# Gated DeltaNet scan on one Trainium2 core: moving outside rows and state scalings from VectorE to GpSimd, and one gram product per direction

## The chip, the cores and the metric

The kernel runs on one core of one Trainium2 chip. The metric is device time in microseconds (us) for one execution of the whole program: both request groups (1024 and 256 tokens) through two layers. Lower is better. A core has TensorE (PE), VectorE (DVE), ScalarE (ACT), GpSimd (POOL) and SyncE (SP), whose queue issues the DMAs here. Each engine works through its own list of instructions in order, and semaphores make one wait for another.

## What is computed

An encoder trunk of two layers. The even layer mixes tokens with four gated DeltaNet heads (A, width 128) and eight RWKV-7 heads (B, width 64), each in both directions; the odd layer uses latent attention; each is followed by an MLP. The change lies in the scan of the even layer. The reference for A, per head, direction and chunk, cut to what matters:

```python
g = jnp.cumsum(g, axis=-1)
decay = jnp.exp(jnp.where(lower, g[..., :, None] - g[..., None, :], -jnp.inf))
L = jnp.where(strict, jnp.einsum('bhnik,bhnjk->bhnij', k_beta, k) * decay, 0.0)
sol = lax.linalg.triangular_solve(eye + L, rhs, left_side=True, lower=True)
u, w = sol[..., :DV], sol[..., DV:]
qk = jnp.einsum('bhnik,bhnjk->bhnij', q, k) * decay
...
v_new = u_c - w_c @ S
o = qd_c @ S + qk_c @ v_new
S = S * jnp.exp(gl_c)[..., None, None] + kd_c.T @ v_new
```

B carries a state of 64x64 per head that is multiplied by a decay per key column at each token and gets two outer products; the kernel also works it in chunks, with exponentials of summed decays on either side.

## The kernel before

All lines below are in `recurrences`, which works the scan in ten turns (`TILES` = 10), unrolled. Turn `i` handles token tile `i` forwards (direction 0) and tile `9 - i` backwards (direction 1), 128 tokens each.

**What a turn holds.** Six groups of four heads each: groups 0 and 1 are A in both directions, 2 to 5 are B. Each needs the inverse of a 128x128 unit triangular matrix per head. The inverse is built from blocks of 2 up to 128 in six levels; both directions of A share one set of tiles (quad 0), B has two sets (quads 1 and 2). For B the levels and quads give 12 units: `unit(u)` is level `u // 2 + 1` of quad `u % 2 + 1`. A unit runs as follows: PE makes Y from the current inverse (`y(u)`), ACT copies it from PSUM (`y_copy(u)`) and copies the inner blocks (`inner(u)`), PE makes the two products Z and ZT (`z(u)`), DVE puts their halves into the inverse (`joins(u)`: L2139, in the last level L2135 and L2136). PE runs `y(u+1)` before `z(u)`; `z(u)` waits for ACT's copy `y_copy(u)`.

**What is fitted between the units.** The lists of the engines are written out by hand. Behind `z(u)` PE does for A: `g_solve` (u = 1, 2), `g_outs` (3, 4), `g_state` for both directions and `g_sums` of the next turn (5), the second `g_sums` (6), the `gram` products (7, 8), and for B two `pairs` of K (9, 10). `g_sums` (L1522) multiplies a matrix of ones with `grow`, which GpSimd writes (L2050), one buffer for both directions: the second `g_rows` waits for the first `g_sums`. After the units come the first inverse of A for the next turn (`g_first`, GpSimd L2058, L2054, L2062, then PE L1569), `right`, `solve` and `outs` of B (PE L1702), between which A's first four levels for the next turn are done.

**The decay of A, before** (for the next turn, units 5 to 8). DVE's `shift` subtracts a row rate from the sums in PSUM (L2119) and adds `outside`, which is 0 inside and -1e9 outside the triangle (L2120). ACT's `decay_exp` takes the exponential in place (L1871). ACT's list has `inner(6)`, `y_copy(6)`, `decay_exp(0)`, `inner(7)`, `y_copy(7)`, `decay_exp(1)`, `inner(8)`, `y_copy(8)`. DVE's `gram` then multiplies, head by head, the K-K product with -beta and the decay into `NTc[0]` (direction 0) or `gY` (direction 1), four instructions at L2129, and the Q-K product with the decay into `A_o` in one (L2132). `gram_used` releases GpSimd's `g_first` and PE's later use of the banks.

**The states.** `S_g` (A) is multiplied by its last decay and gets PE's product, both on DVE (L2220, L2221), at units 5 and 6. `S_r` (B) is multiplied by `e_neg` before `right` reads it (L2252), between DVE's `k_masks(0)` and `k_masks(1)` ahead of unit 0, and by `rest` at the end of `outs` (L2234). DVE's other work here: `g_right` (L2203, L2204), `g_u` (L2208), `g_outs` (L2214 to L2216), `b_masks` (L2174, L2176), `k_masks` (L2183, L2184).

**Own waits.** The helper `Chain` (`link`) makes DVE wait for an instruction of its own that the next one reads. Its count per turn is `PER_DVE`, 40, and `DVE_BEFORE`, 11, ahead of the first turn.

**The prologue.** Ahead of the first turn the same decay and gram are done for turn 0. GpSimd clears tiles, copies the identity and, once all constants have been loaded, makes `first_level` (L2102), then `g_first`. PE waits for `gram_used` before the decay sums of B (L1535).

## Time and profile before

| | before |
|---|---|
| Three runs | 4106.44, 4113.89 (median), 4115.85 us |
| Profiled execution, its own time | 4113.53 us |
| Its span in the profile | 4111.7 us |
| Mean granted clock of TensorE | 0.965 |
| The scan, from its first memsets on GpSimd to the last turn's end | about 684 to 1462 us |
| A steady turn of the scan | 74.68 us |

Times in the rows further down are microseconds from the start of the span. A row of a timeline has the start, the duration, the engine, the line, the operation with output and inputs, the shapes, and the number of instructions put together; in brackets stands how long the engine had been idle and what ended that. Engines start an instruction before the one ahead has fully ended, so the spacing of two starts can be shorter than a duration. PE durations are modelled. Durations of groups elsewhere are means in nanoseconds.

### The profile page before, as it was taken

The page shows a single profiled execution, that of the slowest core. Times are in us where ns is not written, and L with a number is a line of the kernel's source. Part 1 is how long each engine was busy: PE and PEld are TensorE (multiplying, and loading weights), DVE is VectorE, ACT ScalarE, POOL GpSimd, SP SyncE. Part 2 cuts the span into 40 slices and gives each one's busy share as a digit, 9 for nine tenths or more (in the row PEclk, how much of TensorE's full clock was granted, in tenths as well). Part 3 has the DMA queues.
Part 4 walks back from the last instruction along what each step waited for, and adds up shares of the span by engine and source line. Part 5 has one row for each costly group of instructions (what it writes and reads, how often), then busy time and mean ns, then how long its engine had stood idle before and what let it go on. Part 6 is the DMA issues. An engine that isn't in the chain of part 4 may idle for free. (4 is left out here: it accounts for less than half of the span.)

```text
span 4111.7 us, 74086 instructions
## 1 busy us (share of the span) xinstructions
PE 3848.5 (94%) x31096; PEld 3274.5 (80%) x31096; DVE 2130.3 (52%) x3226; ACT 1300.7 (32%) x2303; POOL 897.4 (22%) x473
## 2 busy tenths in 40 slices
PE   7999886999999978999999997899979899999998
PEld 6888864888888867888888886788868788888887
DVE  5643256776777775443333346466643344333335
ACT  4321264444444444111111114255543211111112
POOL 1121065111111123111111112133322211111113
PEclk9999977999999989999999997999999999999999
DMA  4222387122222142011101113000022101110112
GB/s 122 91 77 82 112 289 258 64 78 70 64 90 69 44 175 98 31 41 41 39 32 41 41 41 113 8 7 7 1 77 93 50 32 41 41 39 33 41 41 103
DMA packets 205478, 289.17 MB, mean 70 GB/s; under 512 B 31216, under 2 KB 148144, under 8 KB 205248
## 3 DMA queue, kind: packets, MB, share of 16 engines
q1 hardware_dynamic: 205248, 285.82, 21.0%
q8 instruction: 179, 2.93, 0.3%
q14 instruction: 51, 0.42, 0.0%
HBM read 207.80 MB, written 77.99 MB: 70 GB/s over the span
## 5 line engine op out<-in xcount | busy, mean ns | idle before, releaser
L846 DVE TENSOR_TENSOR top_acc<-top_acc,ffn_down 128x512 f32<-128x512 f32 x600 | 412.1, 687 | 358.7 <-PE ffn_down L111 358.0
L109 PE MATMUL ffn_up<-hT_ffn_high,ffn_w_high 128*128 128x512 f32 (+1 forms) x1536 | 544.0, 354 | 4.9 <-DVE hT_ffn_low L808 4.9
L111 PE MATMUL ffn_up<-hT_ffn_high,ffn_w_low 128*128 128x512 f32 (+1 forms) x1536 | 544.0, 354 | 0.0
L110 PE MATMUL ffn_up<-hT_ffn_low,ffn_w_high 128*128 128x512 f32 (+1 forms) x1536 | 543.7, 354 | 0.0
L109 PE MATMUL ffn_down<-ffn_w_high,ffn_f_high 128*128 128x512 f32 x1280 | 498.6, 390 | 0.0
L110 PE MATMUL ffn_down<-ffn_w_low,ffn_f_high 128*128 128x512 f32 x1280 | 498.3, 389 | 0.0
L111 PE MATMUL ffn_down<-ffn_w_high,ffn_f_low 128*128 128x512 f32 x1280 | 497.9, 389 | 0.0
L835 DVE TENSOR_TENSOR ffn_square<-ffn_relu 128x512 f32<-128x512 f32 (+1 forms) x192 | 146.8, 764 | 640.8 <-ACT ffn_relu L761 640.8
L109 PEld LDWEIGHTS ffn_up<-hT_ffn_high,ffn_w_high 128*128 128x128 f32 x1536 | 290.5, 189 | 46.3 <-issue 5.3
L110 PEld LDWEIGHTS ffn_up<-hT_ffn_low,ffn_w_high 128*128 128x128 f32 x1536 | 290.5, 189 | 41.0
L111 PEld LDWEIGHTS ffn_up<-hT_ffn_high,ffn_w_low 128*128 128x128 f32 x1536 | 290.5, 189 | 40.0
L791 POOL TENSOR_TENSOR ffn_w_low<-up_w_raw,ffn_w_high 128x2048 fp32r<-128x2048 f32 x32 | 147.5, 4610 | 732.9 <-ACT ffn_w_high L767 720.4
L761 ACT ACTIVATE ffn_relu<-ffn_up 128x512 f32<-128x512 f32 (+1 forms) x192 | 101.1, 527 | 634.9 <-PE ffn_up L111 634.9
L753 ACT ACTIVATE ffn_w_high<-up_w_raw 128x2048 fp32r<-128x2048 f32 x32 | 61.4, 1917 | 745.5 <-DVE top_acc L846 695.8
L794 POOL TENSOR_TENSOR ffn_w_low<-up_w_raw,ffn_w_high 128x2048 fp32r<-128x2048 f32 x32 | 147.1, 4596 | 671.1 <-ACT ffn_w_high L753 671.1
L111 PEld LDWEIGHTS ffn_down<-ffn_w_high,ffn_f_low 128*128 128x128 f32 x1280 | 240.3, 188 | 50.2
L109 PEld LDWEIGHTS ffn_down<-ffn_w_high,ffn_f_high 128*128 128x128 f32 x1280 | 240.4, 188 | 49.3
L110 PEld LDWEIGHTS ffn_down<-ffn_w_low,ffn_f_high 128*128 128x128 f32 x1280 | 240.4, 188 | 48.6
L109 PE MATMUL project_bank<-hT_first_high,columns_w_high 128*128 128x512 f32 (+1 forms) x648 | 231.2, 357 | 5.9 <-ACTq L533 3.3
L110 PE MATMUL project_bank<-hT_first_low,columns_w_high 128*128 128x512 f32 (+1 forms) x648 | 230.8, 356 | 0.0
L111 PE MATMUL project_bank<-hT_first_high,columns_w_low 128*128 128x512 f32 (+1 forms) x648 | 230.4, 356 | 0.0
L3144 POOL TENSOR_TENSOR attend_w_sm<-attend_w_sm,attend_inv 128x1024 f32<-128x1024 f32 (+1 forms) x80 | 130.9, 1637 | 179.9 <-DVE attend_inv L3200 179.8
(476 smaller groups left out, 8025.4 us busy)
## 6 DMA issues: line engine op xcount, KB each, us to landing
up_w_raw<-in_w_ff SPq DMA_DIRECT2D x64, 1024.0 KB, 5.1
s_tm_both<-prepare_tb SPq DMA_DIRECT2D x20, 512.0 KB, 7.2
s_fm_dir<-prepare_fd SPq DMA_DIRECT2D x20, 512.0 KB, 5.8
scan_tb<-s_tm_both SPq DMA_DIRECT2D x20, 512.0 KB, 4.0
scan_fb<-s_fm_both SPq DMA_DIRECT2D x20, 512.0 KB, 4.9
scan_fd<-s_fm_dir SPq DMA_DIRECT2D x20, 512.0 KB, 5.2
up_w_raw<-s_x SPq DMA_DIRECT2D x20, 512.0 KB, 4.8
top_acc<-in_w_in_even SPq DMA_DIRECT2D x18, 512.0 KB, 5.4
```

What stands on the lines that cost most here:

```text
L109: pe.matmul(out, stationary[0], moving[0], start=start, stop=False)
L110: pe.matmul(out, stationary[0], moving[1], start=False, stop=False)
L111: return pe.matmul(out, stationary[1], moving[0], start=False, stop=stop)
L753: act.activation(w2_sb[0][:, :, :], w2_raw[:, :, :], ACT.Copy).then_inc(w2_high, 1)
L761: act.activation(relu[u % 2][:, 0:n], bank[u % 4][:, 0:n], ACT.Relu).then_inc(relu_done, 1)
L791: pool.tensor_tensor(w1_sb[1][:, :, :], w1_raw[:, :, :], w1_sb[0][:, :, :].bitcast(F32), ALU.subtract).then_inc(w1_low, 1)
L794: pool.tensor_tensor(w2_sb[1][:, :, :], w2_raw[:, :, :], w2_sb[0][:, :, :].bitcast(F32), ALU.subtract).then_inc(w2_low, 1)
L835: dve.tensor_tensor(square[u % 2][:, 0:n], relu[u % 2][:, 0:n], relu[u % 2][:, 0:n], ALU.mult).then_inc(squared, 1)
L846: dve.tensor_tensor(a, a, out_of(u), ALU.add).then_inc(added, 1)
L3144: pool.tensor_tensor(w_sm[n % (LAG + 1)][:, 0:nk], w_sm[n % (LAG + 1)][:, 0:nk], inv[:, n:n + 1].broadcast_to([P, nk]), ALU.mult).then_inc ...
```

## The change

- The outside rows (`+ outside`) move from DVE to GpSimd (`outside_of`). DVE's `shift` keeps the subtraction and signals `g_moved`; GpSimd waits for that, adds, and signals `g_shift`, for which the exponential waits.
- Behind each exponential ACT waits for its own result and writes `-beta * decay`, head by head (four copies with a scale per partition), into the tile that the gram will fill (`gram_of`: `NTc[0]` or `gY`). DVE then makes the K-K part in one product of 128x512, in place, per direction.
- The scaling of `S_r` by `e_neg` moves to GpSimd (`scale_state`), ahead of the next turn's first `g_rows`; it waits for DVE's multiplications by `rest` of the turn before (`state_rested`). The scaling of `S_g` moves to GpSimd (`scale_g_state`), between the two `g_rows`; it waits for PE's `g_outs`, and DVE's addition waits for it.
- In the prologue GpSimd's two `outside_of` stand behind `first_level`.
- DVE's own waits fall to 25 per turn and 3 before.

The diff, without the list of semaphore names:

```diff
...
     U = [pair[:, :, :, :].rearrange("p a h n -> p (a h n)").rearrange("p (h n) -> p h n", n=P) for pair in (Xp[0], XTp[0])] + [Xp[quad[g]][:, slot[g], :, :] for g in range(2, G)]
     whole_half = [LOWER, UPPER]
+    gram_of = [NTc[0], gY]
     def compact(ap):
...
     X_UNITS = UNITS - RQ
     SUM_CONSTS, SHIFT_CONSTS, CONSTS, CLEARED = 16 * 3, 16 * 4, 16 * 6, 27
-    PER_DVE, DVE_BEFORE = 40, 11
+    PER_DVE, DVE_BEFORE = 25, 3
...
                         pe.wait_ge(s["g_state_used"], 2 * i + 2)
                         gram(i, 1, 0)
                     elif u == 8 and more:
-                        pe.wait_ge(s["g_shift"], 2 * i + 4)
+                        pe.wait_ge(s["g_moved"], 2 * i + 4)
                         gram(i, 1, 1)
                     elif u == 9:
                         if more:
...
                 if more:
                     g_first(i, 1)
-                pe.wait_ge(s["state_scaled"], i + 1)
+                pe.wait_ge(s["state_scaled"], 2 * i + 2)
                 pe.wait_ge(s["k_pairs_used"], 4 * i + 4)
                 for d in range(2):
                     pe.wait_ge(v_in[d], 16 * i + 16)
...
             g_sums(0, 0, 0)
             gram(0, 0, 0)
             g_sums(0, 0, 1)
-            pe.wait_ge(s["g_shift"], 2)
+            pe.wait_ge(s["g_moved"], 2)
             gram(0, 0, 1)
             pe.wait_ge(s["gram_used"], 2)
             for d in range(2):
...
             def decay_exp(i, o, d):
                 act.wait_ge(s["g_shift"], nth(2, i, o, d + 1))
                 act.activation(decay[d][:, :, :], decay[d][:, :, :], ACT.Exp).then_inc(s["g_decay"], 1)
+                act.wait_ge(s["g_decay"], nth(2, i, o, d + 1))
+                if o == 1 and d == 1:
+                    act.wait_ge(s["g_outs_used"], 2 * i + 2)
+                t = tile(d, i, o)
+                for h in range(GH):
+                    last = act.activation(gram_of[d][:, h, :], decay[d][:, h, :], ACT.Copy,
+                                          scale=rates["neg_beta"][d][:, bass.ds(t, 1), h])
+                last.then_inc(s["g_decay_beta"], 1)
             def w_exp(i, o, d):
                 act.wait_ge(s["w_sums"], nth(2, i, o, d + 1))
...
                 pool.tensor_tensor(KD[d][:, :, :], heads(tb[d][:, 0, :]), rate("exp_rest", d, tile(d, i)),
                                    ALU.mult).then_inc(s["kdec"], 1)
+            def outside_of(i, o, d):
+                pool.wait_ge(s["g_moved"], nth(2, i, o, d + 1))
+                pool.tensor_tensor(decay[d][:, :, :], decay[d][:, :, :], bcm(outside[d][:, :], GH),
+                                   ALU.add).then_inc(s["g_shift"], 1)
+
+            def scale_state(i, d):
+                pool.wait_ge(s["state_rested"], 4 * i)
+                pool.wait_ge(s["w_exp"], 2 * i + 2)
+                flat = S_r[d][:, :, :, :].rearrange("p k a n -> p k (a n)")
+                pool.tensor_tensor(flat, flat, bc(e_neg[d][:, :, start_col[d]], P), ALU.mult).then_inc(s["state_scaled"], 1)
+
+            def scale_g_state(i, d):
+                pool.wait_ge(s["g_outs"], 2 * i + d + 1)
+                pool.tensor_tensor(S_g[d][:, :, :], S_g[d][:, :, :], rate("exp_last", d, tile(d, i)),
+                                   ALU.mult).then_inc(s["g_state_scaled"], 1)
+
             def one_turn(i, more):
                 for d in range(2):
                     kdec(i, d)
                 pool.wait_ge(s["rest_made"], 2 * i + 2)
                 for q in range(1, Q):
                     first(i, q)
+                for d in range(2):
+                    scale_state(i, d)
                 if more:
                     g_rows(i, 1, 0)
+                for d in range(2):
+                    scale_g_state(i, d)
+                if more:
                     pool.wait_ge(s["g_sums"], 2 * i + 3)
                     g_rows(i, 1, 1)
+                    for d in range(2):
+                        outside_of(i, 1, d)
                     g_first(i, 1)
             g_rows(0, 0, 0)
...
             pool.wait_ge(s["ident_made"], 1)
             pool.wait_ge(s["consts"], CONSTS)
             pool.tensor_tensor(first_level[:, :], both_levels[:, 0, 0, :], ident_c[:, :], ALU.add).then_inc(s["level_made"], 1)
+            pool.wait_ge(s["shift_consts"], SHIFT_CONSTS)
+            for d in range(2):
+                outside_of(0, 0, d)
             pool.wait_ge(s["cleared"], CLEARED)
             g_first(0, 0)
             for i in range(TILES):
...
                 dve.memset(XTw[q][:, :, :, :], 0.0).then_inc(s["cleared"], 1)
             dve.wait_ge(s["shift_consts"], SHIFT_CONSTS)
-            def shift(link, i, o, d):
+            def shift(i, o, d):
                 t = tile(d, i, o)
                 dve.wait_ge(s["g_sums"], nth(2, i, o, d + 1))
-                link(dve.tensor_tensor(decay[d][:, :, :], heads(ps[:, 4 + d, :]), rate("G", d, t), ALU.subtract))
-                dve.tensor_tensor(decay[d][:, :, :], decay[d][:, :, :], bcm(outside[d][:, :], GH),
-                                  ALU.add).then_inc(s["g_shift"], 1)
+                dve.tensor_tensor(decay[d][:, :, :], heads(ps[:, 4 + d, :]), rate("G", d, t),
+                                  ALU.subtract).then_inc(s["g_moved"], 1)
             def gram(link, i, o, d):
-                t = tile(d, i, o)
-                dve.wait_ge(s["g_decay"], nth(2, i, o, d + 1))
+                dve.wait_ge(s["g_decay_beta"], nth(2, i, o, d + 1))
                 dve.wait_ge(s["gram"], nth(2, i, o, d + 1))
                 v = pairs_view(6 - 2 * d)
-                for h in range(GH):
-                    link(dve.scalar_tensor_tensor((NTc[0][:, h, :], gY[:, h, :])[d], v[:, h, 0, :],
-                                                  rates["neg_beta"][d][:, bass.ds(t, 1), h], decay[d][:, h, :],
-                                                  ALU.mult, ALU.mult))
+                link(dve.tensor_tensor(gram_of[d][:, :, :], v[:, :, 0, :], gram_of[d][:, :, :], ALU.mult))
                 dve.tensor_tensor(A_o[d][:, :, :], v[:, :, 1, :], decay[d][:, :, :], ALU.mult).then_inc(s["gram_used"], 1)
             def last_join(link, q):
...
                 link(dve.tensor_tensor(o, o, R[d], ALU.add))
                 dve.tensor_tensor(o, o, heads(ps[:, 6 + d, :]), ALU.add).then_inc(s["g_outs_used"], 1)
-            def g_state(link, i, d):
+            def g_state(i, d):
+                dve.wait_ge(s["g_state_scaled"], 2 * i + d + 1)
                 dve.wait_ge(s["g_state"], 2 * i + d + 1)
-                link(dve.tensor_tensor(S_g[d][:, :, :], S_g[d][:, :, :], rate("exp_last", d, tile(d, i)), ALU.mult))
                 dve.tensor_tensor(S_g[d][:, :, :], S_g[d][:, :, :], heads(ps[:, 6 + d, :]), ALU.add).then_inc(s["g_state_used"], 1)
             def outs(link, i, g):
...
                     link(dve.tensor_tensor(of_head, of_head, heads(ps[rows, g + 2, 256:384], RN), ALU.add))
                 dve.tensor_tensor(o, o, ps[:, g + 2, 0:4 * RN].rearrange("p (a b n) -> p a b n", a=2, n=RN),
                                   ALU.add).then_inc(s["outs_used"], 1)
-                link(dve.tensor_tensor(state, state, bc(rest[d][:, 2 * half:2 * half + 2, :].rearrange("p k a -> p (k a)"), RN),
-                                       ALU.mult))
+                dve.tensor_tensor(state, state, bc(rest[d][:, 2 * half:2 * half + 2, :].rearrange("p k a -> p (k a)"), RN),
+                                  ALU.mult).then_inc(s["state_rested"], 1)
             def one_turn(i, more):
                 link = Chain(dve, s["dve_chain"], i, PER_DVE, DVE_BEFORE)
...
                 gx(link, i, 0, 5)
                 b_masks(link, i, 3)
                 k_masks(link, i, 0)
-                for d in range(2):
-                    flat = S_r[d][:, :, :, :].rearrange("p k a n -> p k (a n)")
-                    scaled = dve.tensor_tensor(flat, flat, bc(e_neg[d][:, :, start_col[d]], P), ALU.mult)
-                    if d == 0:
-                        link(scaled)
-                scaled.then_inc(s["state_scaled"], 1)
                 k_masks(link, i, 1)
                 for u in range(UNITS):
...
                     elif u < 5:
                         g_outs(link, i, u - 3)
                     elif u == 5:
-                        g_state(link, i, 0)
+                        g_state(i, 0)
                         if more:
-                            shift(link, i, 1, 0)
+                            shift(i, 1, 0)
                     elif u == 6:
-                        g_state(link, i, 1)
+                        g_state(i, 1)
                         if more:
-                            shift(link, i, 1, 1)
+                            shift(i, 1, 1)
                     elif u < 9:
                         if more:
                             gram(link, i, 1, u - 7)
...
             link = Chain(dve, s["dve_chain"])
             for d in range(2):
-                shift(link, 0, 0, d)
+                shift(0, 0, d)
             for d in range(2):
                 gram(link, 0, 0, d)
             b_rows(0, 0, 0)
```

## Rows read from the trace of the kernel before

**Rows 1.** The page, busy time of each engine over the whole span.
```profile
PE 3848.5 (94%) x31096; PEld 3274.5 (80%) x31096; DVE 2130.3 (52%) x3226; ACT 1300.7 (32%) x2303; POOL 897.4 (22%) x473
```

**Rows 2.** Windows: one steady turn; length, PE, PEld, DVE, ACT, POOL, clock, DMA.
```profile
811.44:886.12 74.68, 70.74 (x1516) 61.92 (x1512) 55.31 (x112) 33.18 (x72) 10.41 (x10) 1.00 0.22 73
```

**Rows 3.** Timeline of PE, the same turn, units 5 to 11 and `right`.
```profile
832.60 1.02 PE L1522 MATMUL scan_ps<-scan_grow,scan_ones 128*128 128x512 f32 x2
...
836.15 0.68 PE L1542 MATMUL scan_ps<-scan_X,scan_NT 64*64 64x64 f32 x16
...
836.73 0.68 PE L1549 MATMUL scan_ps<-scan_Y,scan_e_pos 64*64 64x64 f32 x16
...
841.27 1.99 PE L1528 MATMUL scan_ps<-scan_fb 128*128 128x256 f32 x8
...
846.01 0.27 PE L1555 MATMUL scan_ps<-scan_X,scan_NT 64*64 64x64 f32 x1 [0.50 <-DVE scan_X L2139]
...
848.59 0.24 PE L1562 MATMUL scan_ps<-scan_XT,scan_Y 64*64 64x64 f32 x1 [0.57 <-DVE scan_XTw L2136]
...
849.71 0.68 PE L1569 MATMUL scan_ps<-top_ident,scan_gB 64*64 64x64 f32 x16 [0.44 <-POOL scan_gB L2062]
...
850.32 0.44 PE L1702 MATMUL scan_ps<-scan_S_r,scan_AR 128*64 128x128 f32 x4
```

**Rows 4.** Timeline of DVE, the same turn.
```profile
811.44 1.74 DVE L2252 TENSOR_TENSOR scan_S_r<-scan_S_r,scan_e_neg 128x512 f32<-128x512 f32 x2
...
814.93 0.72 DVE L2139 COPY_PREDICATED scan_X<-scan_both_levels,scan_ps 128x256 f32<-128x256 int32 x1 [0.35 <-PE scan_ps L1549]
...
829.27 0.69 DVE L2214 TENSOR_TENSOR scan_gY<-scan_ps,rate_exp_G 128x512 f32<-128x512 f32 x1 [0.70 <-PE scan_ps L1688]
...
831.99 0.68 DVE L2220 TENSOR_TENSOR scan_S_g<-scan_S_g,rate_exp_last 128x512 f32<-128x512 f32 x1
...
834.38 1.00 DVE L2120 TENSOR_TENSOR scan_decay<-scan_decay,scan_outside 128x512 f32<-128x512 f32 x1
...
843.38 1.51 DVE L2129 SCALAR_TENSOR_TENSOR scan_gY<-scan_ps,rate_neg_beta,scan_decay 128x128 f32<-128x128 f32 x4 [0.55 <-PE scan_ps L1528]
844.92 0.69 DVE L2132 TENSOR_TENSOR scan_A_o<-scan_ps,scan_decay 128x512 f32<-128x512 f32 x1
...
849.25 0.73 DVE L2184 COPY_PREDICATED scan_A_ov<-scan_incl,scan_ps 128x512 f32<-128x512 int32 x1
```

**Rows 5.** Timeline of ACT, the same turn.
```profile
835.42 0.63 ACT L1871 ACTIVATE scan_decay<-scan_decay 128x512 f32<-128x512 f32 x1 [5.15 <-DVE scan_decay L2120]
835.96 0.40 ACT L1951 ACTIVATE scan_e_pos<-scan_XT 128x256 f32<-128x256 f32 x1
836.26 0.36 ACT L1955 ACTIVATE scan_Y<-scan_ps 128x256 f32<-128x256 f32 x1
```

**Rows 6.** GpSimd: timeline row, then one line's instructions (ns minimum/median/maximum).
```profile
833.80 1.04 POOL L2050 TENSOR_TENSOR scan_grow<-scan_incl,rate_g 128x512 f32<-128x512 f32 x1 [21.89 <-PE scan_ps L1522]
...
L2062 POOL TENSOR_TENSOR scan_gB<-scan_gB,scan_ident_c x10: 1262/1270/1272, 709.1 to 1377.1; 128x512 f32<-128x512 f32 x10
```

**Rows 7.** Timeline of PE, last turn, y of unit 9.
```profile
1441.05 0.68 PE L1542 MATMUL scan_ps<-scan_X,scan_NT 64*64 64x64 f32 x16 [0.50 <-DVE scan_X L2139]
```

**Rows 8.** Timeline of ACT ahead of the scan: eight activations with a per-partition bias.
```profile
658.12 2.15 ACT L1097 ACTIVATE prepare_a<-prepare_bank,top_acc 128x128 f32<-128x128 f32 x8
```

**Rows 9.** One line of DVE, all its instructions (ns minimum/median/maximum, first and last start).
```profile
L2120 DVE TENSOR_TENSOR scan_decay<-scan_decay,scan_outside x20: 692/848/1057, 693.8 to 1366.7; 128x512 f32<-128x512 f32 x20
```

**Rows 10.** Timeline of the prologue, DVE, GpSimd and PE.
```profile
701.34 0.69 DVE L2132 TENSOR_TENSOR scan_A_o<-scan_ps,scan_decay 128x512 f32<-128x512 f32 x1
...
705.41 0.61 POOL L2102 TENSOR_TENSOR scan_first_level<-scan_both_levels,scan_ident_c 128x64 f32<-128x64 f32 x1 [4.50 <-DMA scan_head_cols<-in_c_head_cols]
...
705.98 1.70 POOL L2058 TENSOR_TENSOR scan_NT<-scan_NT,scan_gY 128x512 f32<-128x512 f32 x1
...
710.42 1.12 PE L1569 MATMUL scan_ps<-top_ident,scan_gB 64*64 64x64 f32 x16 [6.28 <-POOL scan_gB L2062]
```

More of the change, by code:

```diff
@@ L1347, in recurrences @@
     DVE_TILES = 7
-    PER_DVE, DVE_BEFORE = 40, 11
-    names = ("sum_consts", "shift_consts", "consts", "cleared", "g_rows", "g_sums", "g_shift", "g_decay", "gram", "gram_used", "w_sums", "w_exp",
+    PER_DVE, DVE_BEFORE = 25, 3
+    names = ("sum_consts", "shift_consts", "consts", "cleared", "g_rows", "g_sums", "g_shift", "g_moved", "g_decay", "g_decay_beta", "g_state_scaled", "state_rested", "gram", "gram_used", "w_sums", "w_exp",
              "b_rows", "k_rows", "ar_ready", "turned", "turned_out", "b_pairs", "b_pairs_used", "k_pairs", "k_pairs_used",
```

## The prediction

> **What bounds the kernel now.** I read the page first, for busy time: TensorE (PE) is busy 94% of the span, VectorE (DVE) 52% [rows 1]. The change touches the scan alone, ten turns of which nine prepare a next one. So I took the windows view of one steady turn (811.44 to 886.12, 74.68 us): PE 70.74 us busy, DVE 55.31, ScalarE (ACT) 33.18, GpSimd (POOL) 10.41, at the full granted clock of 2.4 GHz [rows 2]. DVE is loaded, but PE is idle for only 3.94 us; whatever DVE gives up, a turn cannot gain more.
>
> Then I laid out the timeline of each engine over the second half of the levels, where nearly all of the edit falls. PE goes without a gap from the decay sum product at 832.60 through y of unit 8 (836.15), z of unit 7 (836.73) and the gram products (the second at 841.27) to about 845.5, then shows three short waits: 0.50 us for DVE's join, 0.57 us for DVE's last join, 0.44 us for GpSimd's first inverse; `right` starts at 850.32 [rows 3]. That start is the yardstick: behind it PE is dense again. In this stretch DVE runs back to back except for short waits on PE's products [rows 4]. ACT waits: the exp starts at 835.42 after 5.15 us of idling, and behind it in ACT's queue stand `inner` and the Y copy of unit 7 (836.26 to 836.62), which PE's z at 836.73 needs [rows 5]. That is the tightest joint: any lengthening ahead of that copy hits PE after about 0.1 us.
>
> **The change, part by part** (steady turn).
>
> *State scalings of RWKV (DVE to GpSimd).* DVE loses 1.74 us from 811.44, but its next join then waits for PE anyway (a wait of 0.35 us at 814.93 already stands [rows 4]), so the gain is 0. GpSimd runs two broadcast multiplies, each like the grow row, 1.04 us [rows 6], by about 813; PE needs them at 850. What queues behind, grow for direction 0, is needed at 832.6. Cost 0; were that cover gone, 2.08 us.
>
> *State scalings of the gated DeltaNet.* DVE loses 0.72 us twice (spacing of the row at 831.99 to the next op [rows 4]). At units 5 and 6 DVE then waits for the sum products, the first of which ends at 833.6 either way [rows 3]: gain 0. GpSimd can start the second when PE's output product ends, which released the DVE row at 829.27 [rows 4], and is through at 830.4, before its second grow at 833.80 [rows 6]; the first is 3.5 us ahead of it. The last turn has no decay work: there the removed op frees PE's 0.50 us wait at 1441.05 [rows 7]: gain 0.5 us once.
>
> *Outside rows.* DVE loses 1.00 us at 834.38 [rows 4] and some 0.69 for the other direction. But the add now stands on GpSimd behind grow, which ends at 834.84 [rows 6]. I price it by GpSimd's in-place add of a repeated tile, 1.27 us [rows 6]: ready at 836.12, where the exp before could start at 835.42 [rows 5]. ACT is 0.7 us later.
>
> *Gram.* DVE's four products of 1.51 us (slot 1.54) become one like the A_o row, 0.69 (slot 0.72): minus 0.82 us, twice [rows 4]. For it ACT gets, between exp and the unit-7 copy, a wait for its own exp (0.63 instead of the 0.54 us spacing, plus 0.04) and four 128x128 copies with a per-partition scale. No such copy is in the scan; the nearest row is eight 128x128 activations with a per-partition bias in 2.15 us, so 0.253 us apart [rows 8]. Below, a copy with a plain scale could be 0.18 (0.54 for 512 columns against 0.30 for 256, extended); above, 0.38, unoverlapped. I take 0.26, as that row has the same shape and one pointer: 1.04 us.
>
> *Sum in the steady turn.* The unit-7 copy moves from 836.26 by 0.70 + 0.13 + 1.04 to about 838.15, is out at 838.5, and PE's z moves from 836.73 to 838.6: **a new stall of 1.87 us**. The direction-1 chain (exp at 838.5, copies to 840.4, unit-8 copy out at 840.9) is met by a PE that is late itself (z of unit 8 at 842.1): no second stall. PE carries the 1.87 to 847.4 for y of unit 11 where it was 846.01 (the 0.50 wait is absorbed). DVE's direction-1 gram product waits for PE (843.38 becomes 845.2) and is 0.82 shorter: the A_o row ends at 846.6 instead of 845.6. GpSimd's three operations with their handoffs, 4.05 us (from the A_o row's end at 845.61 to 849.66, just ahead of PE's 849.71), then end at 850.6 instead of 849.66; DVE's last k mask (849.25 + 0.73) ends near 851.2. PE's `right` starts at 851.3 instead of 850.32: **+0.97 us a turn**. Bounds: +0.25 if all later waits vanish (PE alone), +1.6 with copies of 0.38.
>
> GpSimd's second scaling would overlap DVE's add of two SBUF tiles that follows the row at 829.27. That add and the removed outside row have two SBUF inputs; the latter took 692 ns at least and 1057 at most, the long ones beside a GpSimd grow [rows 9]. Stretching DVE by 0.3 us there delays PE's state product by 0.1 us: +0.1 a turn. So 9 x 1.07 = +9.6 us.
> By the Trainium skill (SBUF — State Buffer, "Who interferes with whom") a VectorE instruction with two SBUF inputs and a GpSimd one that reads SBUF exclude each other, whichever is second waiting for all of the first. By that the delay would be 0.4 us for DVE and 0.15 for PE, 0.5 us more over the scan; the stretched rows agree in kind.
>
> *Prologue.* Before, gram_used came at 702.0 (701.34 + 0.69) while GpSimd was still setting up; its level mask at 705.41 waited for a DMA, and its first inverse was ready at 710.37 [rows 10]. In the change both outside adds stand behind that mask: 706.0 + 2 x 1.27 = 708.6. Then exp and copies for direction 0 end at 709.2, for direction 1 at 711.0, DVE's two products end at 712.4, and GpSimd's three follow by 716.5. PE starts at 716.6 instead of 710.42: **+6.2 us, once**, with 5.5 and 7 as bounds. The sums of the RWKV decay, then at 712.5, run beside GpSimd's part as they do now before it.
>
> No DMA moves: SP waits for the same products. Sum: 9.6 + 6.2 - 0.5 = **+15.3 us**. The profiled execution took 4113.53 us (span 4111.7), within 0.4 of the median of 4113.89. So 4113.5 + 15.3 = 4128.8, given as 4129.
>
> **The rivals.**
> 1. *The queue delay is smaller* (copies at 0.18 us, or the add sooner), so that DVE's saving reaches the end. With no stall the turn gains 0.8 us (join, last k mask and first inverse all come earlier; PE's three waits shrink): 9 x -0.8 + 6.2 - 0.5 = -1.5, 4112. With half a stall about +5. The copy at 836.26, just ahead of its consumer [rows 3, 5], speaks against it. Chance 0.17.
> 2. *Clearly faster: VectorE is what holds PE, everywhere.* DVE sheds 1.69 + 1.74 + 1.44 + 1.64 = 6.5 us a turn; if it turned all of PE's idle time into gain, 9 x -3.94 + 6.2 = -29, 4084. It decides only if ACT's work finishes before 836.6. For it: PE's waits on DVE [rows 3]. Against: most of what is shed lies where DVE waits for PE next. 0.07.
> 3. *GpSimd as a bad neighbour.* If the two engines collide in the outside add too, it takes 1.70 instead of 1.27, as its merge row did in the prologue beside DVE's two-input products [rows 10], and if copies do not overlap (0.38), the turn loses 0.9 more: 9 x 0.9 = 8 more, 4137. Against it: DVE's operations at 835 to 836 read PSUM, and such rows keep their length beside GpSimd. 0.14.
> The Trainium skill (Perfetto Trace Analysis, "Optimizing Scalar/DVE Operations") says that moving work between VectorE and GpSimd might not help, as they share an SBUF read port; that is this rival's ground, and the 1.70 us row is its only witness here.
> 4. Forecast, 0.62.
>
> **How the numbers follow.** A measurement of this kernel can tell about 0.2%, 8.2 us, from nothing: 4105.7 to 4122.1 is "same". Faster is rival 2 and a sliver, 0.08. Same is rival 1 and the forecast's lowest end (9 x 0.25 + 5.5 = +7), 0.18. Slower is the rest, 0.74. The range runs from 4114, which takes in most of rival 1, to 4139, which takes in rival 3 and leaves out rival 2 and a small tail.
>
> **What would show it.** PE's z of unit 7 should wait 1.5 to 2.2 us for ACT's Y copy in nine turns; ACT should show exp, then four copies 0.26 us apart; the turn should be 75.7 us; DVE's busy time in the scan should fall by about 60 us with no gain; the first PE product of GpSimd's inverse should fall near 716.6. I am wrong if PE shows no wait for the Y copy, if the turn gets shorter than 74.7 us, or if the prologue stays within 2 us of now.

## The result, and the profile after

The changed kernel took **4143.5 us** (median of 4 executions, 4136.2 to 4147.3) against 4114.9 for the kernel before on the same chip (4106.4 to 4116.9): ratio **1.0071, 95% interval 1.0051 to 1.0091**. The forecast was slower by 15 us, 4129, with 4139 as the top of its range. The sign was right, the size was half of what came.

The profiled execution took 4136.2 us, span 4134.5. First the page, busy time of each engine in the changed kernel:

```profile
PE 3853.4 (93%) x31096; PEld 3279.7 (79%) x31096; DVE 2083.1 (50%) x3106; ACT 1326.0 (32%) x2383; POOL 963.2 (23%) x533
```

Against [rows 1], DVE sheds 47 us of busy time, and the kernel is slower all the same. PE has the same number of products and 5 us more busy time. That last number looks small, but the work is the same: something made the same products take longer.

Next the windows view of the changed kernel, two turns in a row (a turn is the spacing of GpSimd's merges, the `L2067` rows; the columns are as in [rows 2]):

```profile
780.82:858.38 77.56, 72.26 (x1515) 63.05 (x1509) 50.39 (x99) 35.69 (x81) 16.99 (x15) 0.98 0.21 70
858.38:934.32 75.94, 70.64 (x1515) 62.02 (x1509) 50.28 (x99) 35.72 (x81) 16.99 (x16) 1.00 0.22 72
```

There are two kinds of turn, where [rows 2] had one. The second has the granted clock at 1.00 throughout and is 1.26 us longer than the 74.68 of before. The first has a mean clock of 0.98, PE is busy for 1.62 us more with the same 1515 products, and the turn is longer by just these 1.62 us. Of the nine turns that prepare a next one, six have such a stretch of lower clock (the second, the fourth to seventh, the ninth); some of the later ones are longer still, for a reason taken up below.

The timeline of the changed kernel in the first kind of turn, PE, then ACT, then GpSimd, answers to [rows 3], [rows 5] and [rows 6]; y of unit 8 starts at 846.06 here and at 836.15 there, so 9.91 is to be taken off:

```profile
846.06 0.68 PE L1543 MATMUL scan_ps<-scan_X,scan_NT 64*64 64x64 f32 x16
848.62 0.68 PE L1550 MATMUL scan_ps<-scan_Y,scan_e_pos 64*64 64x64 f32 x16 [1.88 <-ACT scan_e_pos L1960]
...
849.70 3.29 PE L1529 MATMUL scan_ps<-scan_fb 128*128 128x256 f32 x8
...
854.78 1.99 PE L1529 MATMUL scan_ps<-scan_fb 128*128 128x256 f32 x8
...
846.01 0.63 ACT L1872 ACTIVATE scan_decay<-scan_decay 128x512 f32<-128x512 f32 x1 [5.91 <-POOL scan_decay L2087]
846.67 1.28 ACT L1878 ACTIVATE scan_NT<-scan_decay,rate_neg_beta 128x128 f32<-128x128 f32 x4
847.86 0.40 ACT L1960 ACTIVATE scan_e_pos<-scan_XT 128x256 f32<-128x256 f32 x1
848.16 0.36 ACT L1964 ACTIVATE scan_Y<-scan_ps 128x256 f32<-128x256 f32 x1
...
843.71 1.04 POOL L2059 TENSOR_TENSOR scan_grow<-scan_incl,rate_g 128x512 f32<-128x512 f32 x1 [3.53 <-PE scan_ps L1523]
844.71 1.27 POOL L2087 TENSOR_TENSOR scan_decay<-scan_decay,scan_outside 128x512 f32<-128x512 f32 x1
```

Read it from the bottom: grow, the add of the outside rows, the exp, four copies, `inner`, then the Y copy of unit 7, one behind another, and PE's z of unit 7 stands for 1.88 us at the end of this line. That is the stall of the forecast. What the forecast lacks is the next PE row: the eight gram products of direction 0 take 3.29 us, their twins of direction 1 five microseconds later take 1.99, as those of [rows 3] do. The windows view in steps of 1 us shows why (same columns, the eighth is the granted clock):

```profile
847.00:848.00 1.00, 0.00 (x0) 0.00 (x0) 0.00 (x0) 1.00 (x5) 1.00 (x1) 1.00 0.00 0
848.00:849.00 1.00, 0.38 (x13) 0.41 (x15) 0.00 (x0) 1.00 (x3) 0.20 (x1) 1.00 0.00 0
849.00:850.00 1.00, 1.00 (x28) 0.93 (x24) 0.63 (x2) 0.97 (x5) 0.00 (x0) 1.00 0.00 0
850.00:851.00 1.00, 1.00 (x4) 0.86 (x3) 0.26 (x1) 1.00 (x5) 0.00 (x0) 0.62 0.00 0
851.00:852.00 1.00, 1.00 (x4) 0.73 (x3) 0.00 (x0) 1.00 (x3) 0.00 (x0) 0.50 0.00 0
852.00:853.00 1.00, 1.00 (x5) 0.35 (x5) 0.00 (x0) 0.15 (x1) 0.00 (x0) 0.50 0.00 0
853.00:854.00 1.00, 1.00 (x26) 1.00 (x28) 0.86 (x2) 0.03 (x1) 0.00 (x0) 0.68 0.00 0
```

PE stands from 846.74 to 848.62, runs on at the full clock, and then, with PE already fully busy again, the granted clock goes to 0.50 (1.2 GHz) for about 3 us. The fall comes after the wait, not in it.

The kernel before had one such event too, in a turn that neither the rows nor the forecast looked at. Its windows view, the PE row and then windows of 1 us:

```profile
920.36:999.20 78.84, 72.49 (x1508) 63.49 (x1508) 55.48 (x111) 33.19 (x72) 10.40 (x9) 0.98 0.22 69
...
931.98 0.45 PE L1702 MATMUL scan_ps<-scan_NM,scan_XTw 128*64 128x64 f32 x7 [2.40 <-issue]
...
932.00:933.00 1.00, 1.00 (x25) 0.86 (x25) 0.00 (x0) 0.51 (x2) 0.00 (x0) 1.00 0.00 0
933.00:934.00 1.00, 1.00 (x31) 1.00 (x30) 0.00 (x0) 0.86 (x3) 0.00 (x0) 0.82 0.09 16
934.00:935.00 1.00, 1.00 (x22) 0.88 (x19) 0.00 (x0) 0.49 (x2) 0.00 (x0) 0.50 0.03 8
```

PE stood for 2.40 us in the middle of B's `solve` ("issue": the profile shows nothing that it waited for), went on at the full clock, and had half of it from 933.6 for about 3 us. This turn is 4.16 us longer than the 74.68 of a steady one: 2.40 of wait and 1.76 more of busy PE for the same products.

The prologue, from the timeline of the changed kernel, for [rows 10]:

```profile
707.69 2.48 POOL L2087 TENSOR_TENSOR scan_decay<-scan_decay,scan_outside 128x512 f32<-128x512 f32 x2
...
713.51 0.69 DVE L2162 TENSOR_TENSOR scan_A_o<-scan_ps,scan_decay 128x512 f32<-128x512 f32 x1
714.35 1.26 POOL L2067 TENSOR_TENSOR scan_NT<-scan_NT,scan_gY 128x512 f32<-128x512 f32 x1 [4.18 <-DVE scan_A_o L2162]
...
718.35 0.68 PE L1570 MATMUL scan_ps<-top_ident,scan_gB 64*64 64x64 f32 x16 [0.69 <-POOL scan_gB L2071]
```

The first grow starts at 689.19 here; the merge follows 25.16 us later, against 18.82 before: +6.3 us.

### The profile page after: what moved, and what is told of

The parts are those of the page before. It is cut to its first block and busy times, and to the rows that moved or that the text cites. A ratio compares the mean times of both kernels' runs of the same rounds, so it can differ in the third digit from the quotient of the medians.

```text
span 4134.5 us, 74125 instructions
## 1 busy us (share of the span) xinstructions
PE 3853.4 (93%) x31096; PEld 3279.7 (79%) x31096; DVE 2083.1 (50%) x3106; ACT 1326.0 (32%) x2383; POOL 963.2 (23%) x533
```

## The experiments

**Theory.** The loss has three parts, all from the order of work in two queues and none from the work moved. (a) The exp, which comes later because of GpSimd's add, and the four copies stand ahead of the Y copy of unit 7 in ACT's queue: a wait of 1.88 us in each of nine turns. (b) Behind that wait the granted clock falls in most turns: 1.6 us each. (c) In the prologue the outside adds stand behind a DMA wait in GpSimd's queue: 6.3 us once. **Rivals.** GpSimd's added work disturbs VectorE, or the state scalings on GpSimd are late; the clock falls for another reason than the wait; the copies cost by themselves wherever they stand.

A summary first, since the texts refer to each other. Prologue is from the first grow to the first merge; the nine turns are added up; a fall is a turn in which the first gram products run below a granted clock of 1.00. The kernel before took 4112.7, 4112.0, 4111.6 and 4114.6 us in the four groups (A to D) that were run together; the time of each kernel is a median and its ratio is to that of its group.

| kernel | group | us | ratio (95% interval) | prologue | nine turns | PE's wait before z(7) | falls |
|---|---|---|---|---|---|---|---|
| before (profile) | | 4114.9 | | 18.82 | 668.4 | none | 0 |
| changed (profile) | | 4143.5 | 1.0071 | 25.16 | 687.2 | 1.88 | 6 |
| act_order | A | 4111.6 | 0.9996 (0.9986-1.0005) | 25.08 | 658.1 | none | 0 |
| pool_early | A | 4129.3 | 1.0039 (1.0024-1.0054) | 18.33 | 684.0 | 1.88 | 5 |
| both_fixed | A | 4103.9 | 0.9977 (0.9967-0.9988) | 19.12 | 657.5 | none | 0 |
| pe_filled | A | 4131.6 | 1.0048 (1.0033-1.0064) | 25.02 | 684.4 | filled | 0 |
| after_again | B | 4142.6 | 1.0073 (1.0058-1.0087) | 25.04 | 687.3 | 1.88 | 6 |
| pe_filled_8 | B | 4127.9 | 1.0035 (1.0023-1.0047) | 25.04 | 673.7 | filled | 0 |
| gram_undone | B | 4125.7 | 1.0030 (1.0018-1.0041) | 24.74 | 672.8 | 0.58 | 0 |
| states_only | B | 4112.3 | 0.9996 (0.9985-1.0006) | 18.40 | 665.7 | none | 0 |
| outside_undone | C | 4117.7 | 1.0010 (1.0001-1.0019) | 18.97 | 671.0 | 1.20 | 0 |
| fixed_states_back | C | 4107.3 | 0.9987 (0.9978-0.9995) | 18.60 | 659.8 | none | 0 |
| fixed_gram_only | C | 4103.6 | 0.9981 (0.9972-0.9989) | 18.92 | 657.4 | none | 0 |
| wait_only_2 | D | 4140.3 | 1.0064 (1.0046-1.0083) | 18.47 | 696.0 | 1.92 | 7 |

Before's own profile holds the stray turn of 78.84 us shown above among its nine (its fall lies outside the gram products and so is not in the last column); states_only, whose plain turn is within 0.1 us of it, has 665.7 for the nine. In the profiles some of the fourth to ninth turns are longer than the plain one, most of them by a PE wait that the profile puts down to "issue", in B's `solve` or at a product of A's levels behind it (before: 2.40, 0.93 and 0.33 us). Which turns and how much differ from profile to profile, and the cause is not shown. A few microseconds of the nine turns are therefore scatter. The rest of the program, outside the scan, scatters between 3332 and 3345 us from one profile to the next, so steps inside the scan are read from the scan. The scan's time is that from the first grow to DVE's last operation in it.

### act_order: exp and copies one unit later

```
-                    if more and u in (6, 7):
-                        decay_exp(i, 1, u - 6)
+                    if more and u in (7, 8):
+                        decay_exp(i, 1, u - 7)
```

> The changed kernel, with ScalarE's exp and four copies of each direction put one unit later in its list, behind the unit-7 and unit-8 Y copies. Theory (order: the Y copy of unit 7 stands behind the decay work, PE waits 1.88 us and now and then loses its granted clock behind that wait): PE's wait before z of unit 7 is gone, the gram products keep 1.99 us, nine turns take about 661 us where the changed kernel took 687.2 and the kernel before 668.4; the time is 24 to 28 us below the changed kernel's 4143, about 4117; the 6 us of the prologue remain. Rival 1 (ScalarE's amount of work, not its order): the wait reappears at another unit, 0 to 10 us gained. Rival 2 (the clock falls for reasons of its own): only the 1.88 us go, about 17 us gained, and rows of 3 us or more for the gram products are still there.

The nine turns fell from 687.2 to 658.1 us, below both kernels; no wait before z of unit 7, no fall; the prologue stayed at 25.08. One line of order is worth 29 us of the nine turns, so the copies cost nothing where nothing waits behind them, and 7.6 of the 29 lie below the turns of states_only: with the line out of the way the shorter gram on DVE does reach the end. The median is back at the kernel before because the prologue still costs its 6. The gain came out larger than expected: 658.1 for 661, and 4111.6 for about 4117.

### pool_early: the prologue's outside adds ahead of the DMA wait

```
+            pool.wait_ge(s["shift_consts"], SHIFT_CONSTS)
+            for d in range(2):
+                outside_of(0, 0, d)
...
-            pool.wait_ge(s["shift_consts"], SHIFT_CONSTS)
-            for d in range(2):
-                outside_of(0, 0, d)
```

The three lines move from behind the first level mask to right behind the first copies of the identity.

> The changed kernel, with GpSimd's two outside adds of the prologue moved ahead of its tile clearing and the wait for the constants. Theory: the first PE product of GpSimd's inverse comes 6 us earlier relative to the scan's start, and the time falls by 6 us, to about 4137; the nine turns stay as they are (687 us, with waits of 1.88 us). Rival: the clearing that is pushed back, or the start of the clock, takes the gain; 0 to 2 us.

The prologue went to 18.33 us, that of before, and the wait of 1.88 stayed in all nine turns, with a fall in five of them (the second, fourth, sixth, seventh and eighth). (c) stands. The median fell by 14 us against the changed kernel of the first comparison, where 6 were expected. The profiles give 9.2 of them in the scan (790.7 against 799.9: the prologue 6.8 less, the nine turns 3.2 less, half of that the missing fall, the last turn 0.9 more); where the other 5 us of the medians' difference lie is not shown.

### both_fixed: both edits

> Both edits together: the exp and copies one unit later on ScalarE, the prologue's outside adds early on GpSimd. Theory: nine turns in about 661 us and the prologue of the kernel before, so 30 to 34 us below the changed kernel and 5 to 9 us below the kernel before: 4106 to 4110. VectorE's relief is then worth 0.8 us a turn. Rival 1 (the relief is worth nothing once the wait is gone): equal to the kernel before, 4114. Rival 2 (GpSimd as a bad neighbour): above the kernel before by 5 us or more.

4103.9 us: with two pieces of order changed, the change is faster than the kernel before by 0.12 to 0.33%, a little more than expected (nine turns of 657.5 for 661). The timeline of both_fixed, PE and then ACT, shows the joint mended:

```profile
839.96 0.63 PE L1550 MATMUL scan_ps<-scan_Y,scan_e_pos 64*64 64x64 f32 x16
...
840.99 1.99 PE L1529 MATMUL scan_ps<-scan_fb 128*128 128x256 f32 x8
...
839.41 0.63 ACT L1872 ACTIVATE scan_decay<-scan_decay 128x512 f32<-128x512 f32 x1 [1.45 <-POOL scan_decay L2087]
840.07 1.28 ACT L1878 ACTIVATE scan_NT<-scan_decay,rate_neg_beta 128x128 f32<-128x128 f32 x4
...
841.56 0.36 ACT L1964 ACTIVATE scan_Y<-scan_ps 128x256 f32<-128x256 f32 x1
```

The Y copy of unit 7 has already run when the exp starts, and the one behind the copies, of unit 8, is out at 841.92 for a z that PE, with the gram products in between, takes at 843.43.

### pe_filled and pe_filled_8: PE kept busy in the wait

```
+                    if more and u == 7:
+                        for _ in range(8):
+                            pe.matmul(ps[:, 0, 256:384], ident[:, :], ident[:, :], start=True, stop=True)
```

pe_filled has 14 in place of 8. These products are read by nobody.

> The changed kernel with fourteen more 128x128 products on PE ahead of y of unit 8 in nine turns, whose results nobody reads; they fill the time in which PE waits for ScalarE's copy of unit 7. Theory (the idling brings the clock down): z of unit 7 starts as late as in the changed kernel, but no gram product takes more than 2.0 us; the turns with a long gram product lose their 1.5 us each, and the time is 6 to 12 us below the changed kernel although PE does more. Rival (the clock falls whatever PE does there): as many long gram products as in the changed kernel (five or six in nine), no change, or slower by up to 3 us.

> The changed kernel with eight (not fourteen) unread 128x128 products on PE ahead of y of unit 8, 1.83 us by the 0.23 us each took with fourteen, which overfilled the gap by 1 us a turn. Theory (idling brings the clock down): no gram product over 2.0 us, every plain turn at 75.94 us (the changed kernel's own turns without a fall), nine turns in about 676 to 678 us where the changed kernel took 687; the time 9 to 11 us below the changed kernel. Rival (the clock falls whatever PE does): five or six long gram products, no gain.

With 14 the falls were gone, but the products took 3.29 us, more than the wait, and the plain turn grew to 76.96 us: it could not give the size. Its nine turns are only 2.8 us shorter than the changed kernel's, so most of the 12 us by which the median is lower do not come from them. With 8 they fit. The windows view of pe_filled_8 has turns of one kind:

```profile
779.23:855.15 75.92, 72.42 (x1531) 63.95 (x1525) 50.27 (x99) 35.72 (x81) 17.00 (x15) 1.00 0.21 72
855.15:931.06 75.91, 72.42 (x1531) 63.95 (x1525) 50.22 (x99) 35.72 (x81) 17.00 (x15) 1.00 0.22 72
```

75.92 is the turn without a fall of after_again to the hundredth, so everything else of the loss is still there; the nine turns are 13.6 us shorter and the median 14.7. So (b) is the clock, and the clock answers to whether PE stands. Six falls of 1.62 make 9.7 of these 13.6 us; 9 to 11 was expected for the whole. The other 3.9 are not the fill's doing as far as the traces show. The first turn is 1.55 us shorter (65.08 for 66.63): its mean granted clock is 0.94 for 0.88, as the low clock behind the prologue ended sooner, long before the fill is reached. The rest are the "issue" waits: in the changed kernel's first profile 1.11, 0.48, 0.22, 0.14 and 0.18 us in the fourth to eighth turns, which with the falls taken off stay 0.4 to 1.3 us above the plain one.

### after_again: the changed kernel once more

> The changed kernel once more, unedited, beside the kernel before on one chip. Its profiled execution took 4136 us and three more runs 4143 to 4147, while the sibling with the early outside adds took 4129. Theory: the wait of 1.88 us comes in every turn, the fall of the granted clock behind it in five to seven of nine, each worth 1.6 us, so runs scatter between about 4133 and 4145 with a median near 4138; the prologue's 6.3 us are there in each. Rival: the excess over the sibling is a property of the kernel, median 4143 or more.

1.0073 after 1.0071, the same nine turns (687.3), the wait of 1.88 and falls in the same six turns. The median of 4142.6 lies by the rival's 4143 and not by the 4138 of the theory, so the excess of the first comparison repeats.

### gram_undone: the four products back on VectorE, no copies

```
-                for h in range(GH):
-                    last = act.activation(gram_of[d][:, h, :], decay[d][:, h, :], ACT.Copy,
-                                          scale=rates["neg_beta"][d][:, bass.ds(t, 1), h])
...
-                link(dve.tensor_tensor(gram_of[d][:, :, :], v[:, :, 0, :], gram_of[d][:, :, :], ALU.mult))
+                for h in range(GH):
+                    link(dve.scalar_tensor_tensor((NTc[0][:, h, :], gY[:, h, :])[d], v[:, h, 0, :],
...
```

> The changed kernel with the gram as before: no copies on ScalarE, four products a direction on VectorE. Theory: the exp still starts 0.7 us late behind GpSimd's add, so PE waits 0.7 us, not 1.88, before z of unit 7; the turn is 75.4 us, nine turns about 675; the prologue keeps its 6 us; time near 4125. Whether the clock falls behind the shorter wait is open: by the theory that a longer idle is what brings it down, hardly ever. Rival (VectorE is what holds the turn): 5 us slower than the changed kernel, since VectorE works 1.6 us more a turn.

### outside_undone: the outside add back on VectorE

```
-                pool.tensor_tensor(decay[d][:, :, :], decay[d][:, :, :], bcm(outside[d][:, :], GH),
-                                   ALU.add).then_inc(s["g_shift"], 1)
...
+                dve.tensor_tensor(decay[d][:, :, :], decay[d][:, :, :], bcm(outside[d][:, :], GH),
+                                  ALU.add).then_inc(s["g_shift"], 1)
```

> The changed kernel with the outside rows back on VectorE in turns and prologue; gram copies on ScalarE and state scalings on GpSimd stay. Theory: the exp starts 0.7 us sooner, PE's wait before z of unit 7 is 1.2 us; a turn is 75.2 us, 0.5 above the kernel before; the prologue is that of the kernel before (first product of the inverse 23.3 us behind the first grow); some falls of the clock behind a wait of this length, between none and four in nine; 4 to 12 us above the kernel before. Rival (the outside rows had nothing to do with it): wait 1.88 us and 20 us above.

The two undo one delay each, and the waits view (total us, times, longest) gives what is left before z of unit 7, in gram_undone and in outside_undone:

```profile
PE scan_ps L1550 <- ACT scan_e_pos L1952: 5.2, 9, 0.6
```

```profile
PE scan_ps L1550 <- ACT scan_e_pos L1960: 10.8, 9, 1.2
```

0.58 from the outside add alone, 1.20 from the copies alone; together 1.78, against 1.88 measured with both. Neither brings a fall in any of nine turns. With the copies gone but the add on GpSimd the prologue stays at 24.7, with the add on VectorE it is 19.0: (c) belongs to the add. Each half by itself is therefore a small loss (plain turns of 75.43 and 75.24), and the falls come only with both: the two medians lie 13.7 and 6.2 us above before, 19.9 together, and the changed kernel's 30.6, which leaves 10.7 beside the 9.7 of six falls.

### states_only: nothing but the state scalings moved

```
+                for d in range(2):
+                    scale_state(i, d)
...
+                for d in range(2):
+                    scale_g_state(i, d)
```

> The kernel before with the two state scalings alone moved to GpSimd; outside rows and gram stay on VectorE. Theory: worth nothing in a steady turn (74.68 us), at most +0.1 by collision with VectorE's adds, and 0.5 us in the last turn; time within 1 us of the kernel before. Rival (VectorE's load holds the turn): 3.2 us less VectorE work a turn shortens it by 1 us or more, 9 us in all.

Ratio 0.9996, plain turn 74.74. VectorE is busy for 2.6 us a turn less (52.7 for 55.3) and nothing is gained. The rival of GpSimd as a late or bad neighbour is worth 0.06 us a turn here.

### fixed_states_back and fixed_gram_only: how little is needed

The first is both_fixed with the state scalings back on VectorE; the second is the kernel before with the gram part alone and the exp one unit later:

```
-                    if more and u in (6, 7):
-                        decay_exp(i, 1, u - 6)
+                    if more and u in (7, 8):
+                        decay_exp(i, 1, u - 7)
...
-                for h in range(GH):
-                    link(dve.scalar_tensor_tensor((NTc[0][:, h, :], gY[:, h, :])[d], v[:, h, 0, :],
...
+                link(dve.tensor_tensor(gram_of[d][:, :, :], v[:, :, 0, :], gram_of[d][:, :, :], ALU.mult))
```

> The version with both corrections, but with the two state scalings back on VectorE. Theory (VectorE waits for PE where the scalings stood): as fast as the version with both corrections, a turn of 73.8 us, 8 to 9 us below the kernel before, at most 1 us behind its sibling (last turn, collisions). Rival: with ScalarE's wait gone VectorE's load counts, and this one is 5 us or more behind its sibling.

> The kernel before with the gram part alone: exp and four scaled copies a direction on ScalarE, one unit later in its list, one product a direction on VectorE; outside rows and state scalings stay on VectorE. Theory (the gram is the only part that pays): a turn of 73.8 to 73.9 us, as with both corrections, 7 to 9 us below the kernel before. Rival (outside rows off VectorE are needed for it): a turn of 74.3 us or more, under 4 us gained.

fixed_gram_only is 8.0 us below the kernel before, as far as both_fixed, with GpSimd's share of the work as it was. Its steady turn, in the windows view:

```profile
845.00:918.75 73.75, 70.36 (x1515) 61.84 (x1512) 54.03 (x105) 35.93 (x80) 10.42 (x10) 1.00 0.23 74
```

It is 0.93 us shorter than that of [rows 2], with DVE at 54.0 us where both_fixed has 50.3. So 3.8 us less of VectorE work is worth nothing, and the 1.3 us less in the gram products are worth nearly all of themselves. Where it shows on PE, in the timeline of fixed_gram_only:

```profile
847.25 0.24 PE L1563 MATMUL scan_ps<-scan_XT,scan_Y 64*64 64x64 f32 x1 [0.73 <-DVE scan_XTw L2141]
848.20 0.68 PE L1570 MATMUL scan_ps<-top_ident,scan_gB 64*64 64x64 f32 x16 [0.26 <-POOL scan_gB L2071]
```

Of the three waits of [rows 3], 0.50, 0.57 and 0.44, two of 0.73 and 0.26 are left: 0.52 us less. PE's busy time is 0.38 less, which I did not trace further. fixed_states_back took 4107.3, 4.3 us below before where 8 to 9 were expected, and 3.7 above fixed_gram_only. Their intervals overlap and the plain turn is the same (73.76); its nine turns are 2.4 us longer, 1.6 of them in the first turn, most of the rest in "issue" waits (one of 1.83 us in the fourth turn, 1.37 there in fixed_gram_only). Whether the scalings are worth a few tenths of a microsecond elsewhere stays open.

### wait_only_2: the kernel before with the wait alone

```
+                    if more and u == 7:
+                        for n in range(5):
+                            act.activation(spare[:, :], ident[:, :], ACT.Copy,
+                                           scale=rates["neg_beta"][0][:, 0:1, 0]).then_inc(s["spared"], 1)
```

Each copy waits for the one before; nobody reads them. They stand ahead of the Y copy of unit 7.

> The kernel before, with nothing moved, but five unread 128x128 copies with a per-partition scale on ScalarE, each waiting for the one ahead (about 0.42 us apart, 2 us in all), ahead of the Y copy of unit 7. Theory (the wait alone does it): PE waits 1.9 to 2.1 us before z of unit 7; a turn without a fall of the clock is 1.3 to 1.9 us longer (76.0 to 76.6), six to eight of the nine first gram products are longer than 2.2 us behind it and cost 1.6 us each; in all 22 to 28 us above the kernel before, 4134 to 4140, with the prologue untouched. Rival (the moved work on GpSimd and VectorE is what slows the turn or brings the clock down): under 15 us, no long gram products.

PE, timeline, and then two 1-us windows of wait_only_2:

```profile
921.85 0.68 PE L1550 MATMUL scan_ps<-scan_Y,scan_e_pos 64*64 64x64 f32 x16 [1.92 <-issue]
923.08 3.48 PE L1529 MATMUL scan_ps<-scan_fb 128*128 128x256 f32 x8
...
922.00:923.00 1.00, 1.00 (x32) 0.96 (x30) 0.43 (x1) 1.00 (x4) 0.00 (x0) 0.85 0.00 0
923.00:924.00 1.00, 1.00 (x5) 0.84 (x3) 0.46 (x2) 1.00 (x4) 0.00 (x0) 0.50 0.00 0
```

(The profile puts this wait down to "issue", as the Y copy waits for nothing but its turn in ACT's queue.) Nothing was moved between engines, GpSimd and VectorE are as before, and the fall is there in seven of nine turns. A turn with one is 78.34 us, 3.66 above [rows 2]: 1.92 of wait and 1.72 more of busy PE (72.45 for 70.73) for the same products. The two turns without a fall have PE busy for 71.10 us, yet took 78.18 and 78.21, as each has one more "issue" wait of 1.2 us. The median is 25.7 us above before, within the 22 to 28 expected. That settles (b): the wait alone brings it, whatever the rest of the change does.

## Why the prediction was half right

**The yardstick and the place: right.** The forecast took the Y copy of unit 7 for the tightest joint. PE stands before z of unit 7 for 1.88 us, nine times of nine. The forecast's 1.87 is z's delay, from 836.73 to 838.6, and that measured 1.98 (2.56 us after y of unit 8 instead of 0.58), so the two equal figures are luck, and the sum was 0.11 us short.

**The copies: slightly too cheap.** Four took 1.28 us, so (1.28 - 0.38)/3 = 0.30 us apart, where I took 0.26 from the nearest row of equal shape, an activation with a pointer as bias and its input in PSUM [rows 8]. All 40 of them in the changed kernel (minimum, median, maximum in ns):

```profile
L1878 ACT ACTIVATE scan_NT<-scan_decay,rate_neg_beta x40: 384/386/401, 709.6 to 1390.7; 128x128 f32<-128x128 f32 x40
```

The Trainium skill (ScalarE: Activation LUTs, "What ACT_TABLE_LOAD costs") gives 186 ns + 0.833 ns per element for immediate operands, some 93 ns more for each pointer, and an overlap of 93 ns between neighbours: 386 ns for this copy and 293 ns apart. The trace agrees with both, and it would have been the better price. It is worth 0.15 us a turn in ACT's queue, which is the 0.11 above within a few hundredths.

**The turn without a fall: a little too cheap.** 1.07 forecast, 1.26 measured. The copies are 0.1 to 0.15 of the 0.19 between them. The collision of GpSimd's scaling with DVE's two-input add was taken as 0.3 us on DVE: the row is 0.91 instead of 0.69 beside a GpSimd row that still has 0.36 us to run (timeline of the changed kernel, DVE and GpSimd):

```profile
839.82 0.91 DVE L2245 TENSOR_TENSOR top_acc<-top_acc,scan_gY 128x512 f32<-128x512 f32 x1
...
839.14 1.04 POOL L2098 TENSOR_TENSOR scan_S_g<-scan_S_g,rate_exp_last 128x512 f32<-128x512 f32 x1 [2.49 <-PE scan_ps L1689]
```

So DVE lost 0.22 us, and states_only puts this part at 0.06 us a turn. By the rule of the Trainium skill that the forecast quoted (SBUF — State Buffer, "Who interferes with whom"), DVE would have stood until the GpSimd row ended, 0.36 us here; the trace shows it losing less than that.

**The prologue: right.** 6.2 forecast for PE's first inverse product, 5.9 measured there and 6.3 at GpSimd's merge, and pool_early took it away whole.

**The step that failed** is "PE carries the 1.87 to 847.4": it takes TensorE behind the wait as running like TensorE without one. It kept the full clock for a microsecond or so and then had half of it for about 3, in six turns of nine, 1.62 us each. That makes 9.7 us, and it is the term that is missing, put at nothing without a reason. The trace of before had a row for it: its fourth turn, with 2.40 us of wait and 1.76 us of lost speed behind it. The forecast read one steady turn, and none of its rivals had the clock. The sum with the measured terms: 6.3 + 9 x 1.26 + 9.7 - 0.5 = 26.8 us (the 0.5 of the last turn came: PE's waits at `y` for DVE's joins are ten in the scan, 7.3 us in all, and were eleven, 7.8 us). The scan of the changed kernel is 799.9 us, that of states_only, free of before's stray turn, 772.2: 27.7. The medians differ by 28.6 and 30.6 in the two comparisons. The 0.9 between sum and scan and the 1 to 3 between scan and medians are not accounted for; both are within the scatter seen above.

**The rivals.** None of them had the missing term. A smaller queue delay (0.17): not so, the wait came at full length. VectorE as the holder of PE everywhere (0.07): refuted by states_only; the right size of that gain is 0.85 to 0.93 us a turn, from the gram alone, and its condition, that ACT is not in the way, was what act_order met. GpSimd as a bad neighbour (0.14): its add took 1259 to 1274 ns in all 20 cases, not 1.70 us, so the top of the range rested on a price that did not occur, and the measured time went past it for another reason:

```profile
L2087 POOL TENSOR_TENSOR scan_decay<-scan_decay,scan_outside x20: 1259/1266/1274, 707.7 to 1390.1; 128x512 f32<-128x512 f32 x20
```

**The tells.** z's wait, the copies behind the exp and the turn (75.94 without a fall for 75.7) came as written. PE's first inverse product came at 718.35, forecast 716.6: the scan itself began later in this execution, and against the first grow it moved by 5.9 us (29.16 for 23.26). DVE's busy time fell by 47 us instead of 60, as back-to-back operations overlap and the stretched adds gave some back (the two adds of `g_outs` in a plain turn take 1.81 us together, 1.38 before).

## What to carry to other kernels

Before giving a lightly loaded engine more work, ask what stands behind it in that engine's queue: ACT was 44% busy in a turn, and a later exp with four copies of 0.3 us ahead of one short copy cost 29 us over the nine turns, all of it undone by issuing them one unit later. With the prologue's adds moved ahead of their DMA wait as well, a loss of 29 us became a gain of 8. Relieve an engine only where it is the last to end a wait of the one that bounds (here 1.3 us of VectorE's gram work a turn counted and 3.8 us elsewhere did not). And when a forecast puts a new wait of a couple of microseconds into an otherwise dense TensorE, add a term for the clock behind it, and look through all turns of the trace you have, not one, for the longest wait that is already there and what PE's clock did behind it.

## What the runs showed of the hardware

- The granted clock of TensorE fell to 0.50 (1.2 GHz) behind a single wait of 1.88 us amid turns in which PE is 93% busy: full speed through the wait and for 0.3 to 1.6 us of dense work behind it (1.6 in the turn shown of the changed kernel, 0.9 in that of wait_only_2), then some 3 us at half, at a cost of 1.6 to 1.8 us. It came in 17 of 27 turns with 1.88 us (the same six in both profiles of the changed kernel, five in pool_early), in 7 of 9 with 1.92, and behind the one wait of 2.40 in the kernel before. With 1.20 and with 0.58 it came in none of 9 each, in none of 18 when the wait was filled with products that nobody reads, and not behind single waits of 1.37 (fixed_gram_only), 1.76 (gram_undone) and 1.83 us (fixed_states_back). What decides between the turns with and without a fall at the same wait stays open, and between 1.25 and 1.88 us those three single waits are all that the second to ninth turns hold.
- Filling the wait paid even though it added work for the engine that bounds the kernel: with 8 products a turn more, all six falls of 1.62 us were gone, 9.7 us, and nothing was added to the plain turn (75.92 us). The medians differ by 14.7.
- A VectorE add of two SBUF tiles that began with 0.36 us of a GpSimd product of two SBUF tiles still to run took 0.91 us instead of 0.69. Such collisions cost the turn 0.06 us.
